# Order of TensorE's queue in a two-block transformer kernel: dense steps of 8 products, patient mixer steps, RWKV head pairs dealt 3 + 1

## The chip, the cores and the metric

The kernel runs on one core of a Trainium2 chip. The metric is the device time of one execution in microseconds; lower is better. Every time below is of the whole program.

## The reference

512 tokens of width 1024 go through two blocks, all in float32.

Block 1: `h = rmsnorm(x)`, one projection `h @ w_in` (1792 columns for RWKV, 1536 for attention, 2048 for gates). An RWKV-7 mixer works on 8 heads of 64, as four head pairs: a state of 64 x 64 per head is updated token by token,

```
S_t = S_{t-1} diag(w_t) + (S_{t-1} a_t) b_t^T + v_t k_t^T ;  y_t = S_t r_t
```

followed by a group norm, a bonus term and a gate; its result, 512 wide, is `o_a`. A differential attention with 4 heads (two softmaxes of 64-wide queries and keys each, causal, with ALiBi) gives `o_b`. Then

```
merged = sigmoid(g_a) * (o_a @ w_proj_a) + sigmoid(g_b) * (o_b @ w_proj_b)
x = x + merged @ w_out
x = x + square(relu(rmsnorm(x) @ w_ff1)) @ w_ff2          # 1024 -> 4096 -> 1024
x = x + (p @ w_ple) * sigmoid(rmsnorm(x) @ w_ple_gate)
```

Block 2 has the same frame with other mixers: gated linear attention (GLA, 4 heads, keys of 128, values of 256) and a dilated window attention with three groups of 4 heads of 128, merged by their log-sum-exp. A last rmsnorm gives the output.

## The kernel before

**Data.** Activations lie transposed, features on the 128 partitions and 512 tokens along the row. Each dense product is done in float32r in three parts: the weight and the activation are both split into a high and a low half, and `hi*hi`, `hi*lo`, `lo*hi` are summed in one PSUM bank. The halves of activations are called XH and XL (OAH/OAL for the RWKV result, OBH/OBL for the attention result, MH/ML, OGH/OGL, OTH/OTL, mid, YH/YL elsewhere), those of weights wh and wl. Weights come by DMA from SP's queue into two raw buffers (NRAW = 2), ScalarE rounds them into wh (lane "hi"), VectorE subtracts into wl (lane "lo"); there are three buffers of each. Mixer matmuls (scores, transposes against the identity, RWKV and GLA steps) are in plain float32, and the hardware does each of them as more than one matmul record.

**Lanes and steps.** The program is written as generators, one for each chain of work on each engine: a lane. Everything between two `yield`s is a step, the smallest thing that is put into a queue as a whole. TensorE has six lanes (`tensor_lanes`): "norms", "sums", "scores", "a", "b" and "dense". `rehearse` runs every generator once and notes, for each step, its waits, its operations with an estimated duration, and its signals. `arrange` then plays all engines against each other with these estimates: it takes the engine that can start soonest, and of its lanes whose next step is ready the one with the smallest due value. For TensorE that is a fixed priority, norms -7, sums -6, scores -5, a -4, b -3, dense 0. So before the change any mixer step that is ready when a step ends goes ahead of the next dense step. `write` puts the instructions out in the order found. At run time each queue is in order, and an instruction waits only for its semaphores.

**Dense work** (`pe_dense`). A product of one 128-column weight unit with 8 feature slices is 24 matmuls of 128 x 512: `upper` does hi*hi and hi*lo for each slice k, and yields before every second k; `under` does lo*hi and yields before every fourth. A step is thus 4 matmuls. Products with weights of 4 slices (`w_proj_a`, `w_proj_b`) have 12. `tm`, which is used where the result must have tokens on partitions (values for the attentions, and the last gate), has steps of 6. The order of products in block 1 is: RWKV columns, attention values, queries and keys of two heads, gates, queries and keys of the other two, gates; then pairs of gate products ("gb") alternating with products of the attention result OBH, OBL ("pb"); then the four of the RWKV result OAH, OAL ("pa"); then `w_out`, the MLP, the gate.

**RWKV.** `pe_prep` has six to eight steps for each of the four head pairs (LD,LS; bones; ident; rkw; AR,BT), in lanes a and b by turns. A block inverse on VectorE follows. Then two workers (`pe_worker`, lanes a and b, each with two PSUM banks and eleven pages of its own) go through items: one item is one head pair and one half of the tokens. In an item TensorE does, in this order and each waiting for an evacuation of the one before: AR,KT (two steps), AR,BT (two), transposes ident,AR and ident,V, the last item's output (ident,T or ident,SQ, with GD,G), transposes ident,BT and ident,KT, VT,AKR, then X,UB, G,NB, X,UB, then ARB,UA with BP,UA, then UA,BP with VT,KP, then up to four state steps SB,MP, and the output UA,ARB, VT,AKR, SB,AR. Most of these use 64 rows or 64 columns of the array. The items are in `WORK` (line 21): pairs 0 and 1 for worker 0, pairs 2 and 3 for worker 1. Worker 0 waits for the inverse. Worker 1 uses pages and banks of the attention and waits for its end: `at("l", "OB", 3)`, which is the last OBL, and the last score's maximum.

**Attention.** `pe_scores` has 32 steps (AQ, 64 rows, 128 to 512 columns), all in one bank, each waiting until VectorE has taken the last. `pe_sums` transposes the probabilities (ident,AP) and multiplies by the values (AV,PT); `pe_attn_norm` (ident,scan) turns a finished head. In block 2 `pe_gla_prep`, `pe_gla_mix`, `pe_dil_scores` (DQ) and `pe_dil_sum` (ident,P and PTD,DVT) are in the same lanes.

Of the kernel before, what the change touches and what calls it, by code (L numbers as in the profile page):

```python
# [17 lines left out]
NEG = -3.0e38  # L18
C_DECAY = float(np.exp(-0.5))
GN_EPS = 64 * 1e-5  # L20
WORK = ((0, 1), (2, 3))
# [199 lines left out]
class Lane:  # L221
    def __init__(self, stream, name, write, slack):
        self.stream, self.name, self.write, self.slack = stream, name, write, slack
        self.steps, self.unit_of, self.i, self.gen = [], [], 0, None


class Kernel:
# [162 lines left out]
    def upper(self, s, u, j, x, key, k0, k1):  # L390
# [4 lines left out]
        for k in range(k0, k1):  # L395
            if k % 2 == 0 and k > k0:
                yield
            w = u["hi"][:, k, 128 * j:128 * j + 128] if both is None else both[:, k, :]
            o = bank[:, :] if both is None else bank[0:48, :]
            pe.wait_ge(self.at("hi" if both is None else "lo", u["i"]), self.at("h", x, k))  # L400
            pe.matmul(o, w, self.x[x][0][k], k == 0, False)
            pe.wait_ge(self.at("l", x, k))
            i = pe.matmul(o, w, self.x[x][1][k], False, both is not None and k == u["kk"] - 1)
            self.mm += 2
            if both is not None and k == u["kk"] - 1:
                i.then_inc(*s.up(("acc",) + key, ("wfree", u["i"])))

    def under(self, s, u, j, x, key, k0, k1):
# [3 lines left out]
        for k in range(k0, k1):  # L412
            if k % 4 == 0:
                yield
# [626 lines left out]
    def pe_prep(self, s, i):  # L1041
        pe, bank = self.pe, self.ps[4 + i % 2]
# [161 lines left out]
    def pe_worker(self, s, w):  # L1204
        pe, b, at = self.pe, self.W[w], self.at
# [325 lines left out]
    def pe_scores(self, s):  # L1531
        pe, bank = self.pe, self.ps[6]
        last = [("begin", 6)]
# [45 lines left out]
    def pe_sums(self, s):  # L1579
        pe, at, bank, ob = self.pe, self.at, self.ps[7], self.ps[3]  # L1580
        free = [("begin", 7)]
# [774 lines left out]
    def pe_gla_prep(self, s, h):  # L2356
        pe = self.pe
        yield
# [58 lines left out]
    def pe_gla_mix(self, s):  # L2417
        pe, at, bank = self.pe, self.at, self.gla_bank
        for h in range(4):
# [119 lines left out]
    def pe_dil_scores(self, s):  # L2539
        pe, at = self.pe, self.at  # L2540
        for g in range(3):
# [321 lines left out]
    def rehearse(self):  # L2863
        for eng, stream, lanes in (("pe", self.pe, self.tensor_lanes), ("dv", self.dv, self.vector_lanes), ("ac", self.ac, self.scalar_lanes),
                                   ("pl", self.pl, self.pool_lanes), ("sp", self.sp, self.sync_lanes)):
            self.order[eng] = []
            for name, slack, write in lanes():
                self.splitting = 0
# [3 lines left out]
                while more:  # L2872
# [6 lines left out]
                    lane.unit_of.append(self.splitting)  # L2879
                self.lanes.append(lane)  # L2880
# [4 lines left out]
    def arrange(self):  # L2885
# [26 lines left out]
        while any(left.values()):  # L2912
# [9 lines left out]
            start, eng, go = best  # L2922
# [9 lines left out]
            lane = min(go, key=due)[1]  # L2932
            now, stream = start, streams[eng]
            for note in lane.steps[lane.i]:
# [85 lines left out]
```

## Time and profile before

| | |
|---|---|
| runs shown | 1953.95, 1956.66, 1958.48 us; median 1956.66 |
| profiled execution | 1953.57 us, its span from first to last instruction 1951.8 us |
| TensorE busy, mean granted clock | 1928.2 us, 0.997 |
| TensorE's weight loads (beside its matmuls) | 1580.0 us |
| VectorE, ScalarE, GpSimdE busy | 1017.2, 738.6, 99.9 us |
| matmul records | 9550 |

The duration of one matmul in the rows (389 ns for a dense one) is from its start to its end in a pipeline: the next starts before it ends. What a stretch costs is read from starts. "x4" in a timeline row is a group of neighbours of one kind, its first start and the time to its last end. Mixer tiles are named by what they hold; buffer numbers are left out, so both workers' tiles have one name (the output page is T for worker 0, SQ for worker 1).

### The profile page before, as it was taken

What the parts mean: (1) busy time and instruction counts of PE and PEld (TensorE: products, weight loads), DVE (VectorE), ACT (ScalarE), POOL (GpSimd) and SP (SyncE); (2) the same over time, 40 slices, a digit from 0 to 9 for tenths busy, and PEclk for the clock granted to TensorE, in tenths of its full rate; (3) what the DMA queues carried; (4) which work ended last, traced back from release to release, by engine and by line L of the source; (5) the groups of instructions that cost most, each with busy time, mean ns of one, the idle gap of its engine ahead of it and who ended that gap; (6) DMA issues with size and microseconds to landing.
All of it is one profiled execution on the core that took longest, in us unless ns stands there. A gap on an engine that the chain in (4) does not pass through costs nothing.

```text
span 1951.8 us, 23333 instructions
## 1 busy us (share of the span) xinstructions
PE 1928.2 (99%) x9550; PEld 1580.0 (81%) x9550; DVE 1017.2 (52%) x1717; ACT 738.6 (38%) x1184; POOL 99.9 (5%) x155
## 2 busy tenths in 40 slices
PE   7999999999999999999999999999999999999997
PEld 6787778778888888888788888898888888888886
DVE  5768574446754444466834435424345644444544
ACT  6434454333433223234734233333233432313233
POOL 2000111102000000000101000000000000000000
PEclk9999999999999999999999999999999999999999
DMA  6232310226343233232432222231354332322321
GB/s 223 65 103 95 82 46 29 65 76 234 102 149 99 96 97 98 96 99 76 142 98 64 74 80 84 91 107 64 110 194 141 97 108 87 108 86 87 108 87 43
DMA packets 174557, 194.65 MB, mean 100 GB/s; under 512 B 14825, under 2 KB 151699, under 8 KB 174450
## 3 DMA queue, kind: packets, MB, share of 16 engines
q1 hardware_dynamic: 167794, 179.82, 28.8%
q0 software_dynamic: 5072, 11.03, 1.7%
q10 hardware_dynamic: 1584, 2.30, 0.3%
q8 instruction: 76, 1.25, 0.3%
q14 instruction: 31, 0.25, 0.0%
HBM read 179.41 MB, written 15.54 MB: 100 GB/s over the span
## 4 chain that ended last, share of the span: by engine, by line
PE 95%; DVE 2%; ACT 2%; DMA 1%; issue 0%; POOL 0%; ACTq 0%; POOLq 0%; DVEq 0%
PE bank L130 93%; PE bank L133 2%; ACT L140 0%; DMA scr_x<-XT 0%; DVE XL L162 0%; DVE XT L162 0%; ACT GP L140 0%; DVE wl L154 0%; DMA g_rows<-in_norm_mix_g_dram 0%; ACT xt L140 0%; DVE KI L154 0%; DVE GP L162 0%; ACT LD L140 0%; DVE GP L177 0%; POOL scr_x L118 0%
## 5 line engine op out<-in xcount | busy, mean ns | idle before, releaser
L140 ACT ACTIVATE wh<-raw 128x1024 fp32r<-128x1024 f32 (+1 forms) x299 | 316.0, 1057 | 709.7 <-PE bank L130 706.0
L130 PE MATMUL bank<-XH,wh 128*128 128x512 f32 (+1 forms) x1272 | 507.7, 399 | 3.0 <-DVE XL L162 2.2
L130 PE MATMUL bank<-XL,wh 128*128 128x512 f32 (+1 forms) x1272 | 497.0, 391 | 0.0
L154 DVE TENSOR_TENSOR wl<-raw,wh 128x1024 fp32r<-128x1024 f32 x298 | 365.2, 1226 | 228.6 <-ACT wh L140 227.9
L130 PE MATMUL bank<-XH,wl 128*128 128x512 f32 x1264 | 324.3, 394 | 0.0
L130 PEld LDWEIGHTS bank<-XH,wh 128*128 128x128 f32 (+1 forms) x1272 | 239.1, 188 | 60.4 <-issue 5.2
L130 PEld LDWEIGHTS bank<-XL,wh 128*128 128x128 f32 (+1 forms) x1272 | 239.2, 188 | 47.9
L130 PEld LDWEIGHTS bank<-XH,wl 128*128 128x128 f32 x1264 | 233.5, 188 | 51.9 <-issue 4.1
L130 PE MATMUL bank<-mid,wh 128*128 128x512 f32 x1024 | 243.8, 389 | 0.0
L130 PEld LDWEIGHTS bank<-mid,wh 128*128 128x128 f32 x1024 | 192.2, 188 | 39.9
L154 DVE TENSOR_TENSOR T<-bank,RST 128x512 f32<-128x512 f32 x122 | 84.1, 689 | 234.2 <-PE bank L130 234.0
L130 PE MATMUL bank<-mid,wl 128*128 128x512 f32 x512 | 127.7, 389 | 0.0
L130 PEld LDWEIGHTS bank<-mid,wl 128*128 128x128 f32 x512 | 96.1, 188 | 20.0
L154 DVE TENSOR_TENSOR T<-T 128x512 f32<-128x512 f32 (+1 forms) x68 | 45.1, 673 | 88.2 <-ACT T L140 88.1
L140 ACT ACTIVATE T<-bank 128x512 f32<-128x512 f32 x64 | 37.1, 592 | 115.2 <-PE bank L130 115.2
L130 PE MATMUL bank<-wh,XH 128*128 128x512 f32 x192 | 60.3, 395 | 0.0
L130 PE MATMUL bank<-wl,XH 128*128 128x512 f32 x192 | 59.8, 392 | 0.0
L130 PE MATMUL bank<-wh,XL 128*128 128x512 f32 x192 | 59.7, 392 | 0.0
L154 DVE TENSOR_TENSOR XT<-XT,T 128x512 f32<-128x512 f32 x72 | 49.8, 691 | 2.1
L130 PE MATMUL bank<-OGH,wh 128*128 128x512 f32 x128 | 50.1, 391 | 0.0
L130 PE MATMUL bank<-OGL,wh 128*128 128x512 f32 x128 | 49.8, 389 | 0.0
L154 DVE TENSOR_TENSOR T<-T,bank 128x512 f32<-128x512 f32 (+1 forms) x40 | 26.3, 658 | 41.0 <-PE bank L130 26.0
(426 smaller groups left out, 2319.3 us busy)
## 6 DMA issues: line engine op xcount, KB each, us to landing
raw<-in_w_in_dram SPq DMA_DIRECT2D x58, 1024.0 KB, 5.3
raw<-in_w_ff_dram SPq DMA_DIRECT2D x32, 1024.0 KB, 5.3
raw<-in_w_mlp_dram SPq DMA_DIRECT2D x32, 1024.0 KB, 5.3
raw<-in_w_out_dram SPq DMA_DIRECT2D x8, 1024.0 KB, 5.6
scr_x<-XT POOLq DMA_DIRECT2D x16, 256.0 KB, 4.9
XT<-scr_x SPq DMA_DIRECT2D x8, 512.0 KB, 8.0
raw<-in_w_ple_gate_dram SPq DMA_DIRECT2D x4, 1024.0 KB, 5.3
raw<-in_w_o_gla_dram SPq DMA_DIRECT2D x4, 1024.0 KB, 5.3
```

The source lines that it names most:

```text
L130: return self.put(ns, lambda e: e.matmul(out, lhsT, rhs, start=start, stop=stop, skip_group_check=True))
L133: return self.put(109, lambda e: e.transpose(out, in_, ident))
L140: return self.put(ns, lambda e: e.activation(out, in_, func, bias=bias, scale=scale), func)
L154: return self.put(self.ns(out), lambda e: e.tensor_tensor(out, a, b, op))
```

## The change

Four things are changed, all of them in what the planner is given or how it picks.

- `upper` yields before every fourth k and `under` before every eighth, so a dense step of a product on 8 slices is 8 matmuls. `tm` is as it was.
- Every step of a TensorE lane has a patience, noted at the rehearsal: `PATIENCE = (2000, 4000, 0)` ns, the first for attention in block 1 (scores and sums), the second for the mixers of block 2, the third for the RWKV preparation; 0 for the workers and the norms. If TensorE's last step was dense and a dense step is ready, the dense one is taken as long as every other ready step has been ready for less than its patience. Once a mixer step has been taken the old rule holds: mixer steps go on as long as one is ready.
- The planner adds 90 ns to TensorE's clock at each change between dense and mixer steps. This is in the plan only, no instruction is issued.
- `WORK` gives pairs 0, 1 and 3 to worker 0 and pair 2 to worker 1.

```diff
--- before.py
+++ after.py
@@ -16,9 +16,10 @@
 BASE = 16512
 PAGE = 2048
 NEG = -3.0e38
+PATIENCE = (2000, 4000, 0)
 C_DECAY = float(np.exp(-0.5))
 GN_EPS = 64 * 1e-5
-WORK = ((0, 1), (2, 3))
+WORK = ((0, 1, 3), (2,))
 C128 = 128.0 ** -0.5
 LAM_INIT = 0.8 - 0.6 * float(np.exp(-0.3 * 0))
 
@@ -221,7 +222,7 @@
 class Lane:
     def __init__(self, stream, name, write, slack):
         self.stream, self.name, self.write, self.slack = stream, name, write, slack
-        self.steps, self.unit_of, self.i, self.gen = [], [], 0, None
+        self.steps, self.unit_of, self.patience, self.i, self.gen = [], [], [], 0, None
 
 
 class Kernel:
@@ -393,7 +394,7 @@
         if k0 == 0:
             pe.wait_ge(*[self.at(*e) for e in self.bank_after[key]])
         for k in range(k0, k1):
-            if k % 2 == 0 and k > k0:
+            if k % 4 == 0 and k > k0:
                 yield
             w = u["hi"][:, k, 128 * j:128 * j + 128] if both is None else both[:, k, :]
             o = bank[:, :] if both is None else bank[0:48, :]
@@ -410,7 +411,7 @@
         if k0 == 0 and j == 0:
             self.need_lo[u["i"]] = self.mm
         for k in range(k0, k1):
-            if k % 4 == 0:
+            if k % 8 == 0:
                 yield
             pe.wait_ge(self.at("lo", u["i"]))
             i = pe.matmul(bank[:, :], u["lo"][:, k, 128 * j:128 * j + 128], self.x[x][0][k], False, k == u["kk"] - 1)
@@ -1039,6 +1040,7 @@
             dv.tensor_tensor(self.LL[r[x], :], self.WA[r[x], :], self.LD[x][r[x], :].bitcast(F32), ALU.subtract).then_inc(*s.up(("ll",)))
 
     def pe_prep(self, s, i):
+        self.patient = PATIENCE[2]
         pe, bank = self.pe, self.ps[4 + i % 2]
         pb, cs = self.prep_pages[i % 2][1], slice(128 * i, 128 * i + 128)
         for x, (name, free) in enumerate((("zw", ("abe", i - 2, 1) if i >= 2 else ("pv",) if i == 0 else ("rst0",)), ("za", ("sg", i)))):
@@ -1202,6 +1204,7 @@
         return [(i, hf) for i in self.W[w]["todo"] for hf in range(2)]
 
     def pe_worker(self, s, w):
+        self.patient = 0
         pe, b, at = self.pe, self.W[w], self.at
         ARB, AKR, BP, KP, VT, MP, X, G, UA, UB, NB, SB = [b[n] for n in ("ARB", "AKR", "BP", "KP", "VT", "MP", "X", "G", "UA", "UB", "NB", "SB")]
         B0, B1 = b["banks"]
@@ -1530,6 +1533,7 @@
 
     def pe_scores(self, s):
         pe, bank = self.pe, self.ps[6]
+        self.patient = PATIENCE[0]
         last = [("begin", 6)]
         for h, b in self.items:
             n = 128 * (b + 1)
@@ -1578,6 +1582,7 @@
 
     def pe_sums(self, s):
         pe, at, bank, ob = self.pe, self.at, self.ps[7], self.ps[3]
+        self.patient = PATIENCE[0]
         free = [("begin", 7)]
         for x in range(17):
             if x < 16:
@@ -2355,6 +2360,7 @@
 
     def pe_gla_prep(self, s, h):
         pe = self.pe
+        self.patient = PATIENCE[1]
         yield
         pe.wait_ge(self.at("hasl"), self.at("free", "ha"), self.at("wasl"), *([self.at("p1", h - 2)] if h >= 2 else [self.at("browc", h)]))
         pe.matmul(self.ps[6 + h % 2][:, :], self.WAS[:, 128 * h:128 * h + 128], self.HAS[:, :], True, True).then_inc(*s.up(("zb", h)))
@@ -2416,6 +2422,7 @@
 
     def pe_gla_mix(self, s):
         pe, at, bank = self.pe, self.at, self.gla_bank
+        self.patient = PATIENCE[1]
         for h in range(4):
             vs = slice(256 * h, 256 * h + 256)
             yield
@@ -2538,6 +2545,7 @@
 
     def pe_dil_scores(self, s):
         pe, at = self.pe, self.at
+        self.patient = PATIENCE[1]
         for g in range(3):
             for h in range(4):
                 qk = self.DQ[h % 2]
@@ -2865,7 +2873,7 @@
                                    ("pl", self.pl, self.pool_lanes), ("sp", self.sp, self.sync_lanes)):
             self.order[eng] = []
             for name, slack, write in lanes():
-                self.splitting = 0
+                self.splitting = self.patient = 0
                 lane = Lane(eng, name, write, slack)
                 sig, gen = self.sig(f"{eng}_{name}"), None
                 gen, more = write(sig), True
@@ -2877,6 +2885,7 @@
                         more = False
                     lane.steps.append(stream.notes)
                     lane.unit_of.append(self.splitting)
+                    lane.patience.append(self.patient)
                 self.lanes.append(lane)
         self.rehearsing = False
         for sig in self.sigs.values():
@@ -2930,7 +2939,15 @@
                     return max(t, clock["pe"]) + 227 * (need[l.unit_of[l.i]] - dense) - lead
                 return t + l.slack
             lane = min(go, key=due)[1]
+            if eng == "pe":
+
+                was = self.order[eng][-1] if self.order[eng] else lane
+                dense_lane = [l for _, l in go if l.name == "dense"]
+                if was.name == "dense" and dense_lane and all(start - t < l.patience[l.i] for t, l in go if l.name != "dense"):
+                    lane = dense_lane[0]
             now, stream = start, streams[eng]
+            if eng == "pe" and (lane.name == "dense") != (was.name == "dense"):
+                now += 90
             for note in lane.steps[lane.i]:
                 if note[0] == "wait":
                     sem, value = place[note[1]] if note[2] is None else (note[1].name, note[2])
```

## Rows read from the trace of the kernel before

**Rows 1.** The page: its first line, TensorE's busy share, its granted clock by slice.

```profile
span 1951.8 us, 23333 instructions
...
PE 1928.2 (99%) x9550; PEld 1580.0 (81%) x9550; DVE 1017.2 (52%) x1717; ACT 738.6 (38%) x1184; POOL 99.9 (5%) x155
...
PEclk9999999999999999999999999999999999999999
```

**Rows 2.** Waits of TensorE over the span: us in total, times, longest.

```profile
PE bank L133 <- DMA g_rows<-in_norm_mix_g_dram: 5.1, 1, 5.1
```

**Rows 3.** TensorE's timeline, end of the RWKV mixer: start us, us, what.

```profile
447.36 0.39 PE L130 MATMUL bank<-OBH,wh 128*128 128x512 f32 x1
...
450.10 0.39 PE L130 MATMUL bank<-OBH,wh 128*128 128x512 f32 x1
...
456.22 0.39 PE L130 MATMUL bank<-OAH,wh 128*128 128x512 f32 x1
```

**Rows 4.** TensorE's timeline from 308 us: worker 0's state steps between dense runs.

```profile
311.78 0.33 PE L130 MATMUL bank<-SB,MP 64*64 64x64 f32 x4
...
313.17 0.33 PE L130 MATMUL bank<-SB,MP 64*64 64x64 f32 x4
```

**Rows 5.** TensorE's timeline from 337 us: a state step between other worker steps.

```profile
338.54 0.33 PE L130 MATMUL bank<-SB,MP 64*64 64x64 f32 x4
338.80 0.34 PE L130 MATMUL bank<-UA,BP 128*64 128x64 f32 x4
```

**Rows 6.** TensorE's timeline from 281 us: dense matmuls between two score steps.

```profile
283.75 0.50 PE L130 MATMUL bank<-XH,wh 128*128 128x512 f32 x1
...
285.79 1.12 PE L130 MATMUL bank<-AQ 64*128 64x512 f32 x2
```

**Rows 7.** TensorE's timeline in block 2, from 1044 us.

```profile
1046.79 1.03 PE L130 MATMUL bank<-GV,KOT 128*128 128x256 f32 x4
1047.47 0.58 PE L130 MATMUL bank<-XH,wh 128*128 128x512 f32 x1
...
1049.51 0.59 PE L130 MATMUL bank<-GV,KOT 128*128 128x256 f32 x2
1049.94 1.04 PE L133 MATMUL bank<-ident,T 128*128 128x128 f32 x8
```

**Rows 8.** Tiles OBH, OBL and OAL: ns min/median/max, first and last start, forms.

```profile
L130 PE MATMUL bank<-OBH,wh x32: 387/396/583, 377.4 to 454.9; 128*128 128x512 f32 x32
...
L162 DVE SCALAR_TENSOR_TENSOR OBL<-bank,sg,OBH x4: 741/745/753, 215.0 to 303.2; 128x512 fp32r<-128x512 f32 x4
...
L154 DVE TENSOR_TENSOR OAL<-SQ,OAH x4: 424/426/426, 365.8 to 456.0; 128x256 fp32r<-128x256 f32 x4
```

**Rows 9.** TensorE's timeline: AR,KT at the start of three items of worker 1.

```profile
314.56 0.54 PE L130 MATMUL bank<-AR,KT 64*64 64x128 f32 x5
...
385.29 0.65 PE L130 MATMUL bank<-AR,KT 64*64 64x128 f32 x8
...
415.78 0.65 PE L130 MATMUL bank<-AR,KT 64*64 64x128 f32 x8
```

**Rows 10.** TensorE's groups by form from 211 to 456 us: busy us, mean ns.

```profile
L130 PE MATMUL bank<-XH,wh 128*128 128x512 f32 x120 | 51.2, 426 | 0.0
...
L130 PE MATMUL bank<-OBH,wl 128*128 128x512 f32 x32 | 9.1, 405 | 0.0
```

**Rows 11.** Tiles SS and OTL: first and last start.

```profile
L130 PE MATMUL bank<-SS,QD x24: 379/379/379, 1033.0 to 1064.4; 128*128 128x256 f32 x24
...
L154 DVE TENSOR_TENSOR OTL<-bank,OTH x4: 690/692/692, 1321.1 to 1359.9; 128x512 fp32r<-128x512 f32 x4
```

**Rows 12.** TensorE from 14 to 16 us: us, busy (count), granted clock, DMA.

```profile
14.00:16.00 2.00, 2.00 (x7) 0.50 1.13 325
```

## The prediction

> **What bounds the kernel now.** I read the page's busy shares and slices first, then TensorE's waits, then TensorE's timeline around its changes of work, and last the tiles that carry work from one stage to the next. TensorE is busy in 99% of the span, in every slice after the first, at full granted clock [rows 1]. Its waits are a handful, all but one in the first microseconds or in block 2, the longest 5.1 us [rows 2]. So the time is the work in TensorE's queue plus what it loses where it changes from one kind of work to another. Of its 9550 matmuls 7264 are dense ones, which start every 0.227 us when they follow each other (twelve of them from 447.36 to 450.10 us take 2.74, 0.228 each [rows 3]). That is 1649 us. I call the runs of other matmuls between them excursions; counted in TensorE's timeline over the whole span there are 174.
>
> What does an excursion cost beyond its matmuls? It depends on its kind.
> - A state step of a worker, SB,MP (64 x 64), alone between dense runs: a step at 311.78, the next at 313.17 [rows 4]. One period is 313.17 - 311.78 = 1.39 us, of which four dense matmuls are 0.91, which leaves 0.48. The same step between steps of its own kind takes 338.80 - 338.54 = 0.26 us [rows 5]. So leaving and coming back costs 0.22 us.
> - A score step, AQ (64 rows): eight dense matmuls from 283.75 to 285.79 take 2.04 us where 8 x 0.227 = 1.82 [rows 6]: 0.22 us again.
> - A step on the whole array (128 rows and columns) in block 2: eight dense from 1047.47 to 1049.51 take 2.04 us, again 0.22 too long, but the step before them, four matmuls of 256 columns, takes only 1047.47 - 1046.79 = 0.68 where its own pitch (1049.51 to 1049.94: two in 0.43) gives 0.86 [rows 7]. The sum is 0.22 - 0.18 = 0.04 us.
>
> I take 0.21 us for an excursion with half-array steps and 0.04 for one without. By my count in the timeline 87 of the 174 hold a half-array step: 14 in the RWKV preparation (37 to 135 us), 16 in attention alone (162 to 211), 32 while worker 0 runs (211 to 348), 25 after that. All of block 2's are whole-array. What the excursions cost is therefore about 87 x 0.21 + 87 x 0.04 = 21.8 us, 1.1% of the time. That is a ceiling; no edit here removes a matmul.
>
> The rows also show why. The Trainium skill (TensorEngine Tiling (Array Packing), Key Properties) says that a change of tiling mode drains TensorE, while another tile of the same mode doesn't. By that rule the price is on changes of mode and not on excursions, and patience in block 2, where no mode changes, buys nothing; the trace agrees (0.04 against 0.22 us). At a flat 0.18 us for each excursion, as the planner books it now (90 ns each way), block 2's part below would be 4.5 us and not 1.
>
> **The change part by part.** Matmuls, their operands, the DMAs and the other engines' instructions stay; what changes is the order in each queue, TensorE's above all.
>
> *Dense steps of 8.* A dense product on 8 slices was six steps of 4 matmuls and is three of 8. The planner can leave it at half as many places: a worker step that is ready after 4 matmuls now waits for 8, up to 0.91 us more. It removes an excursion only where two ready steps fall into one gap. Row-major products (tm) keep their steps of 6. The 90 ns that the planner adds to its clock at each change of kind issue nothing; they only shift what it takes for ready, which I price at 0, within 1 us either way.
>
> *Patience.* In block 1 a score or sums step waits until it has been ready for 2.0 us if the planner is in dense work and nothing else is due; in block 2 all mixer steps wait 4.0 us; preparation, workers and norms don't wait. From 162 to 211 us only attention runs: the score steps come 2.5 to 3.5 us apart on average; with a wait of 2.0 us and steps of 1.82 us they come two dense steps and their own 0.4 to 1.1 us apart, about 4.9 us. So 49 us hold some 10 excursions for 16, which saves 6 x 0.21 = 1.3 us; four of the 32 score steps slide behind 211 us, where they ride along with worker steps.
>
> *Pairs 3 + 1.* Worker 1 can't start before attention ends, as its pages and banks are attention's: the last OBL is written at 303.2 to 303.9 us [rows 8] and its first AR,KT is at 314.56 [rows 9]. Now it has four half-pair items in series, the last of which is normalised into OAL at 456.0 to 456.4; the product that needs it starts at 456.2 [rows 3, 8]. From 348 us on worker 1 runs alone, in 25 half-array excursions. After the change worker 0 goes on with pair 3 beside worker 1's pair 2: two items beside each other took 7 excursions between 314.5 and 348 us, one alone takes 12 (counted from its first step at 385.29 to the next item at 415.78 [rows 9]; 8 of the 12 are half-array). So the 25 become 6 + 8, and a few for norms, about 15: 10 x 0.21 = 2.1 us.
>
> *Sum.* Preparation: two or three of 14 merge as two lanes share it, 0.5 us; attention 1.3; 211 to 348 us: 32 to about 29, 0.6; after that 2.1. Half-array excursions go from 87 to some 66, 4.5 us. Whole-array ones (11 to 40 fewer, most in block 2) save 25 x 0.04 = 1.0 us at most, and I take 0.3, since those with a half-array neighbour still pay its price. In all 4.8 us. The bounds: 1 us if merging pairs half-array with whole-array steps only, 8 us if 40% of the half-array excursions go and most of block 2's too.
>
> **Does a wait take its place?** The dense work is what fills TensorE while a mixer step is evacuated. From 211.3 to 456.2 us there are 124 + 2 x 120 + 3 x 32 = 460 dense matmuls, in six rows of which the first and the last stand in [rows 10]. They then meet two gates.
> - *OBH, OBL at 377.4 us* [rows 8] need attention's end, at 303.9 now: 73 us of slack. Afterwards attention ends later: four score steps late at 4 to 5 us each, and longer gaps, so about 320 to 335 us. The gate comes sooner, since the 268 dense matmuls before it go by in runs of 8: some 35 are done already by 211 us (the mixers' 4 to 5 us that slid, and 3 us of later preparation), and the other 233 are 29 runs, which at 3.7 to 4.5 us each with their excursion give 321 to 345 us. The slack is nearly gone; I price a miss at 0 to 6 us of idle.
> - *OAH, OAL at 456.2 us* need the last worker item and its norm. Item alone: 30.5 us from 385.29 to 415.78 [rows 9], of it 68 dense matmuls (15.4 us) in 12 runs, seven of 4 and five of 8. With every run at 8 it is 15.1 + 12 x 1.82 = 36.9 us. From 211 to 314.5 us there are 35 runs and 176 matmuls; at 8 each for all, 280, 24 us more. The pair of items beside each other: 33.5 us with 7 runs, 5.7 us more. End of the chain at the worst: 211 + 3 (preparation) + 103 + 24 + 2 x 39 + 37 + 10 (norm) = 466 us. But that takes no run away; long runs let more steps get ready, and a run that bridges a latency already is not made longer. With a third of the added time gone that way (24 + 11 + 6 = 41 becomes 27) it is 452. The dense work alone gets there at 456.2 - 4.5 = 451.7. So the two meet, as they do now with 1 us between them. Because the matmuls behind the gate don't depend on any of this, only the gate's moment counts: idle is 0 to 11 us.
>
> In block 2 the waits lengthen chains with room: GLA's mix has its last SS,QD at 1064 and OGH is first used at 1334; OTL is written by 1360 and the first OTH product is at 1431.7 [rows 11].
>
> Queued behind: SP's loads of the alibi page wait for a head's scores, and the next weight loads stand behind them; POOL's memsets for worker 1 wait for the last OBL, with the norm powers of worker 0 behind. If attention is later than the planner has it, both queues stand. I price it at 0, covered by two raw weight buffers, each of which lasts two units, 48 x 0.227 = 10.9 us, and at 3 us if that cover is gone.
>
> **How the time comes out.** Profiled execution before: span 1951.8, its time 1953.57, of which 1.8 lies around the span. 1953.57 - 4.8 + 0.3 for idle at the second gate = 1949.1. The median of the runs shown is 1956.66, 3.1 above the profiled one: 1952.2, so 1952.
>
> **Rivals.**
> 1. *The gates eat it.* Idle of 2 to 6 us at either gate, savings of 3 to 5: 1954 to 1960, mostly within 0.2% (3.9 us, about what a measurement of this kernel tells from no change). For it: both slacks shrink to a few us by the sums above. Against: worker steps don't wait by the rule, and the 3 + 1 deal takes two items off the late starter.
> 2. *Slower: the RWKV chain holds the product on OA.* Six items in series on worker 0, each 6 us longer, end at 462 to 466 us; the gate opens 6 to 10 us after 456.2 and everything behind it moves by that. 1956.7 + 6 to 10 = 1963 to 1967. It decides as soon as the last OAL is later than about 460 us, that is if less than a seventh of the 41 us above is saved by merging. For it: 12 runs per item are forced by the chain itself. Against: in the trace of before two items side by side need hardly more dense work than one. An idle TensorE could also lose clock: from 14 to 16 us, after the first waits, the granted clock was 0.50 (the lower level, 1.2 GHz) and the 2 us held five dense starts (the row counts two more that were under way), where 0.227 us apart it would be nine [rows 12]; I give that 1 to 2 us more.
> 3. *Nothing merges.* Half- and whole-array steps meet, so the changes of mode stay: 1 us saved, 1955 to 1956. The Trainium skill's rule on tiling modes (TensorEngine Tiling (Array Packing), Key Properties) is for this one.
>
> **Chances.** Forecast case (saving 4 to 8, no gate late) 0.47; gates eat it 0.21; nothing merges 0.11; slower by the chain or the OB gate 0.21. Faster than 0.2% 0.47, same 0.32, slower 0.21. The range 1944 to 1963 takes in 8 us saved, with room for the scatter of the medians (the three runs shown lie 4.5 us apart), and the slower case's lower end; about 0.09 lies above and 0.08 below. The likeliest case alone: 1946 to 1953.
>
> **What would show it.** Right: excursions down from 174 to about 125 to 140, those with half-array steps to about 66; AQ steps mostly two dense steps apart before 211 us; worker 0's KT,AR running on to about 410; TensorE's busy share 99% with no wait over 1 us at the first OBH or OAH. Wrong: a wait of TensorE on OBL or OAL or on a step of the worker between 320 and 460 us, OAH starting after 456.2, or a dense pitch other than 0.227 us.

## The result, and the profile after

| | before | after |
|---|---|---|
| median | 1956.66 us (1953.95 to 1958.48, 5 runs) | 1948.59 us (1947.35 to 1952.46, 5 runs) |
| profiled execution, span | 1953.57, 1951.8 us | 1947.35, 1945.5 us |

The ratio is 0.9963, 95% interval [0.9948, 0.9978]: faster, by 8.1 us in the medians and by 6.3 us in the two profiled spans. The forecast was a median of 1952 us. Executions of one kernel lie up to 10 us apart (r3's 16), so below the lowest time of a kernel stands beside its median. One execution of e1, at a mean granted clock of 0.751, took 2399.5 us and is left out of every comparison.

The page after, its first line, TensorE's busy share and its granted clock by slice, against [rows 1]: the same number of matmuls, the same clock, 6.3 us less of busy TensorE.

```profile
span 1945.5 us, 23335 instructions
...
PE 1921.9 (99%) x9550; PEld 1582.4 (81%) x9550; DVE 1018.8 (52%) x1717; ACT 740.1 (38%) x1186; POOL 97.8 (5%) x155
...
PEclk9999999999999999999999999999999999999999
```

Waits of TensorE after (us in total, times, longest), against [rows 2]. The first and longest one is the one of before. None names a tile of either gate, OBL or OAL.

```profile
PE bank L134 <- DMA g_rows<-in_norm_mix_g_dram: 5.3, 1, 5.3
PE bank L131 <- DVE XL L163: 2.2, 1, 2.2
PE bank L134 <- DVE AP L163: 1.3, 2, 0.9
```

TensorE's timeline at the end of the mixer stretch, against [rows 3]. Twelve dense matmuls take 451.01 - 448.29 = 2.72 us, 0.227 each as before; the first product on OAH starts at 451.01 where it started at 456.22.

```profile
448.29 0.39 PE L131 MATMUL bank<-OBH,wh 128*128 128x512 f32 x1
...
451.01 0.39 PE L131 MATMUL bank<-OAH,wh 128*128 128x512 f32 x1
```

So 5.2 of the 6.3 us are gained ahead of that product, although the first matmul of all starts 0.25 us later than before (5.34 and 5.09 us). Behind it before took 1951.8 - 456.2 = 1495.6 us and after 1945.5 - 451.0 = 1494.5: the other 1.1 us, in block 2.

The tiles at the two gates (ns min/median/max, first and last start), against [rows 8]. The last OBL starts at 306.2 us and the first OBH product at 370.6: 64 us of room. The last OAL starts at 437.3 and takes 0.4, and its product starts at 451.0: 13 us of room, where before had none (456.0 and 456.2).

```profile
L131 PE MATMUL bank<-OBH,wh x32: 387/389/497, 370.6 to 449.6; 128*128 128x512 f32 x32
...
L163 DVE SCALAR_TENSOR_TENSOR OBL<-bank,sg,OBH x4: 746/748/753, 218.1 to 306.2; 128x512 fp32r<-128x512 f32 x4
...
L155 DVE TENSOR_TENSOR OAL<-T,OAH x6: 418/424/428, 250.9 to 437.3; 128x256 fp32r<-128x256 f32 x6
```

TensorE's timeline, AR,KT of the first item of worker 0, of the first of worker 1 and of the last item of all, against [rows 9]. Worker 0 begins at 200.0 us (before: 211.3), worker 1 at 316.4 (314.6).

```profile
200.00 0.68 PE L131 MATMUL bank<-AR,KT 64*64 64x128 f32 x16
...
316.35 0.68 PE L131 MATMUL bank<-AR,KT 64*64 64x128 f32 x16
...
394.93 0.71 PE L131 MATMUL bank<-AR,KT 64*64 64x128 f32 x12
```

TensorE's timeline in attention alone: the score steps now stand mostly 16 dense matmuls apart, 4.3 to 4.9 us from one to the next (the last two before 200 us are 6.7 and 3.1 us apart).

```profile
166.61 0.48 PE L131 MATMUL bank<-AQ 64*128 64x128 f32 x2
...
170.99 0.70 PE L131 MATMUL bank<-AQ 64*128 64x256 f32 x2
171.62 0.50 PE L131 MATMUL bank<-XH,wh 128*128 128x512 f32 x1
...
175.49 0.70 PE L131 MATMUL bank<-AQ 64*128 64x256 f32 x2
```

Counted in TensorE's timeline as before, excursions fall from 174 to 115, those with half-array steps from 87 to 62:

| us | half-array excursions before | after |
|---|---|---|
| 37 to 135 | 14 | 13 |
| 162 to 211 | 16 | 11 |
| 211 to 348 | 32 | 23 |
| 348 to 446 | 25 | 15 |

By the prediction's prices that is 25 x 0.21 + 34 x 0.04 = 6.6 us, against 6.3 measured.

The mixers of block 2 (first and last start), against [rows 11]: later by 17 and 34 us, and still ahead of the products that need them; OTL is read from 1425.7 us on.

```profile
L131 PE MATMUL bank<-SS,QD x24: 379/379/379, 1036.2 to 1081.4; 128*128 128x256 f32 x24
...
L155 DVE TENSOR_TENSOR OTL<-bank,OTH x4: 691/692/693, 1318.5 to 1393.6; 128x512 fp32r<-128x512 f32 x4
```

### The profile page after: what moved, and what is told of

Same layout as the page of the kernel before. It is cut to its first block, busy times and chain, and to the rows that moved or that the text cites. A ratio compares the mean times of both kernels' runs of the same rounds, so it can differ in the third digit from the quotient of the medians.

```text
span 1945.5 us, 23335 instructions
## 1 busy us (share of the span) xinstructions
PE 1921.9 (99%) x9550; PEld 1582.4 (81%) x9550; DVE 1018.8 (52%) x1717; ACT 740.1 (38%) x1186; POOL 97.8 (5%) x155
## 4 chain that ended last, share of the span: by engine, by line
PE 96%; ACT 2%; DVE 1%; DMA 1%; issue 0%; POOL 0%; ACTq 0%; DVEq 0%
PE bank L131 94%; PE bank L134 2%; DMA scr_x<-XT 0%; ACT L141 0%; DVE XL L163 0%; ACT GP L141 0%; DMA g_rows<-in_norm_mix_g_dram 0%; DVE wl L155 0%; ACT wh L141 0%; ACT xt L141 0%; POOL scr_x L119 0%; ACT LD L141 0%; ACT AP L142 0%; DVE KI L155 0%; ACT T L141 0%
## 5 line engine op out<-in xcount | busy, mean ns | idle before, releaser
L131 PE MATMUL bank<-XH,wl 128*128 128x512 f32 x1264 | 317.7, 392 | 0.0
```

The costliest lines, as they stand in the source:

```text
L131: return self.put(ns, lambda e: e.matmul(out, lhsT, rhs, start=start, stop=stop, skip_group_check=True))
```

## The experiments

Three questions: is the price on the change between half and whole array (the prediction's account) or on every excursion; which of the edits brings the gain; and how near is the kernel to the chain of RWKV items (rival 2)? Twelve runs; kernels in one table part ran on one chip beside the kernel before.

The expectations name accounts of the price by letters. A: 0.21 us for an excursion with half-array steps, 0.04 for one without, as predicted. B: a flat 0.107 us for each. C: the deal alone is worth nothing. D: the price is on each change between half-array and whole-array matmuls. In r1 to r4, which were written last, "A" is what D was, at 0.2 us a change, and "A0" is the A of before.

| kernel | median us | lowest us | ratio to before, 95% |
|---|---|---|---|
| before (23 runs) | 1954.72 | 1952.37 | |
| e1: before, pairs 3 + 1 | 1952.69 | 1949.48 | 0.9986 [0.9977, 0.9995] |
| e2: before, dense steps of 8 | 1961.63 | 1961.36 | 1.0040 [1.0028, 1.0052] |
| e3: after, pairs 2 + 2 | 1961.38 | 1959.15 | 1.0034 [1.0021, 1.0047] |
| e4: after, no patience | 1948.01 | 1947.41 | 0.9973 [0.9961, 0.9985] |
| before (1 run) | 1956.07 | | |
| q1 to q4: probes | 2069.44, 2123.20, 2070.47, 2175.30 | | one run each |
| before (17 runs) | 1956.08 | 1952.46 | |
| r1: after again | 1948.17 | 1946.60 | 0.9964 [0.9952, 0.9977] |
| r2: scores wait 5 us | 1946.71 | 1945.57 | 0.9957 [0.9945, 0.9969] |
| r3: workers wait 2 us | 1992.37 | 1981.36 | 1.0181 [1.0156, 1.0206] |
| r4: without the 90 ns | 1956.43 | 1953.76 | 1.0006 [0.9995, 1.0016] |

### What an excursion costs: q1 to q4

Each adds the same 1024 matmul records of 128 columns (512 matmuls, whose results are overwritten) to the kernel before, in the MLPs, where there are no mixers: on 128 rows of the identity (q1, q3) or 64 rows (q2, q4); four matmuls at one place of a product, or two at two places. q2 against q1 has 128 half-array excursions for 128 whole-array ones; q3 and q4 have 256.

```
+    def probe(self, u, n):
+        if u["name"] in ("f1", "f2"):
+            for x in range(n):
+                self.pe.matmul(self.ps[3][:, 128 * x:128 * x + 128], self.ident[0:64, :], self.ident[0:64, :], x == 0, True)   # q1, q3: 0:128
+            self.mm += n
...
             if k % 4 == 0:
                 yield
+            if k == 0:
+                self.probe(u, 4)      # q3, q4: 2 here and 2 in upper at k == 4
```

> A measurement of the price itself: the kernel before, with four extra plain float32 matmuls of 128 x 128 by 128 (identity by identity, into a bank that nobody reads then) in each of the 128 products of the two MLPs, ahead of its lo*hi part; their result is not used. All use the whole array. In the mixers such a group of four takes 0.91 us and costs 0.01 to 0.1 on leaving and coming back. Theories A and D: span longer by 128 x (0.90 + 0.02) = 117 us. Flat price of 0.107 (theory B): 128 x (0.90 + 0.107) = 128 us.

> As the whole-array probe, but with 64 of the 128 rows: four matmuls of 64 x 128 by 128 at each of the 128 places. Theory B: as long as with the whole array. Theories A and D: longer than it by the price of a half-array excursion, 128 x 0.21 = 27 us, or up to 128 x 0.38 = 49 us if the AR,BT steps of the preparation show it (8 records in 1.29 us, against 0.91 for 8 on the whole array).

> As the whole-array probe with the same number of extra matmuls, but dealt to two places in each product, two and two (256 excursions for 128). Theories A and D: 128 x 0.04 = 5 us longer than all four at one place, or less. Theory B: 128 x 0.107 = 14 us longer.

> As the half-array probe, dealt two and two. This is gathering undone, 128 times. Theories A and D: 27 to 49 us longer than all four at one place. Theory B: 14 us longer.

Spans, one execution each: q1 2067.7, q2 2121.4, q3 2068.7, q4 2173.5 us (the kernel before beside them 1954.3). q1 is 113.4 us longer, where A and D said 117 and B 128. q2 - q1 = 53.7 us for 128 excursions made half-array, 0.42 each. q4 - q2 = 52.1 for 128 more half-array ones, 0.41 each. q3 - q1 = 1.0 for 128 more whole-array ones, 0.008 each. The spans also differ ahead of the probes: the first product on OAH starts at 456.07, 457.75, 455.54 and 455.74 us. From there to the end the same differences are 52.1, 54.1 and 1.5 us, or 0.41, 0.42 and 0.012 each. The half-array price lies above the widest expectation (0.38). A flat price is refuted: an excursion that stays on the whole array is nearly free here. TensorE's timeline shows one of each. In q1:

```profile
705.95 1.05 PE L130 MATMUL bank<-ident 128*128 128x128 f32 x8
706.76 2.07 PE L130 MATMUL bank<-XH,wl 128*128 128x512 f32 x8
708.67 0.39 PE L130 MATMUL bank<-XH,wh 128*128 128x512 f32 x1
```

708.67 - 705.95 = 2.72 us is just 8 x 0.113 + 8 x 0.227. In q2, counted from the last dense matmul before it:

```profile
705.10 0.39 PE L130 MATMUL bank<-XL,wh 128*128 128x512 f32 x1
705.42 1.16 PE L130 MATMUL bank<-ident 64*128 64x128 f32 x8
706.51 2.11 PE L130 MATMUL bank<-XH,wl 128*128 128x512 f32 x8
708.46 0.39 PE L130 MATMUL bank<-XH,wh 128*128 128x512 f32 x1
```

3.36 us for 0.227 + 2.72 = 2.95: 0.41 too much, spread over the way in (705.10 to 705.42: 0.09 over a pitch), the first steps inside, and the way out. The price of the prediction, 0.21, was half of that. The reason is in its yardstick: the 0.26 us of a state step "between steps of its own kind" [rows 5] ran from SB,MP (64 x 64) to UA,BP (128 x 64), another form, and held a change itself. TensorE's timeline of e4 has eight state matmuls as one group,

```profile
350.64 0.45 PE L131 MATMUL bank<-SB,MP 64*64 64x64 f32 x8
```

0.45 us from first start to last end where four take 0.33 [rows 5]: 0.12 for four more. With that in place of 0.26 the excursion of [rows 4] costs 1.39 - 0.91 - 0.12 = 0.36. The prediction's second case, the score step, had the same gap: [rows 6] was read on the dense side alone, and what the step itself loses was left out, though it was counted for block 2. In the changed kernel two AQ matmuls of 256 columns hold TensorE from 170.99 to 171.62, 0.63 us, where two of 256 columns on the whole array take 0.43 [rows 7]: 0.20 too long. The 16 dense ones up to 175.49 take 3.87 us where 16 x 0.227 = 3.63: another 0.24. Together that is 0.44.

Why then does 0.21 fit the change (6.6 against 6.3)? Two errors cancel. Counted in TensorE's timeline ahead of the first product on OAH, the changes between dense and half-array matmuls fall from 142 to 92, which is 25 round trips. But those between half-array and whole-array mixer steps, inside the excursions, rise from 109 to 139: a merged excursion often holds both. (Changes between two unlike half-array forms stay, 31 and 34.) So 10 round trips go on balance, 4.1 us at 0.41. The planner's order says the same, 252 changes between half and whole array before and 232 after.

The starts bear this out. Summed from each start to the next, the 1104 dense matmuls ahead of that product take 277.3 us before and 268.4 after, 8.9 less; the mixer matmuls between them take 173.9 and 177.3, 3.4 more. That makes 5.5 us, of which the 10 round trips are 4.1. The other 1.4 us, and the 1.1 in block 2, go along with 34 fewer whole-array excursions, 0.07 us each. That is a remainder and not a measured price; q3 has 0.012 for such an excursion of identity matmuls.

### The parts alone: e1, e2, e3

**e1**, the kernel before with the new deal only (150 excursions, 74 half-array, by its order; 174 and 88 before).

```
-WORK = ((0, 1), (2, 3))
+WORK = ((0, 1, 3), (2,))
```

> The kernel before, with the 3 + 1 deal of the head pairs alone (dense steps of 4, no patience). Counted in TensorE's queue as it is written, excursions go from 174 (88 with half-array steps, 86 without) to 150 (74 and 76). Theory A, a price of 0.21 us for an excursion with half-array steps and 0.04 for one without: 14 x 0.21 + 10 x 0.04 = 3.3 us less. Theory B, a flat price for every excursion (the change took 59 away for 6.3 us of span, 0.107 each): 24 x 0.107 = 2.6 us less. Theory C, that the deal only repairs what the longer dense steps break and is worth nothing alone: 0. OAH's first matmul: 3 us sooner than 456.2 by A, with the last OAL far earlier than now.

2.0 us under before in the medians, 2.9 in the lowest times. There is no trace of it at full clock, so only its times are used. They refute C. They fit A (14 x 0.21 + 10 x 0.04 = 3.3) and B (2.6) alike: the interval spans 1.0 to 4.5 us.

**e2**, the kernel before with the new dense steps only (144 excursions, 72 half-array).

```
-            if k % 2 == 0 and k > k0:
+            if k % 4 == 0 and k > k0:
...
-            if k % 4 == 0:
+            if k % 8 == 0:
```

> The kernel before, with dense steps of 8 alone (old deal, no patience). Excursions 144 (72 with half-array steps, 72 without) for 174 (88, 86). Theory A without idle: 16 x 0.21 + 14 x 0.04 = 3.9 us less. Theory A with my rival 2, that four items in series on worker 1 after attention's end reach the product on OA late: each item 6 us longer, 317 + 4 x 36.9 + 10 = 475 us for the last OAL against about 452 for the dense work, less what merges, so 8 to 20 us of idle before OAH's first matmul, and the time 4 to 16 us above before. TensorE's waits in the trace decide between them.

Its excursions promised 3.9 us (16 x 0.21 + 14 x 0.04); it is 7 to 9 us slower instead. This is rival 2. TensorE's timeline of e2 has the last dense group of the stretch at 443.89, then the last item's steps with nothing between them, then the norm:

```profile
443.89 1.17 PE L130 MATMUL bank<-OBH,wl 128*128 128x512 f32 x4
444.90 1.08 PE L130 MATMUL bank<-G,NB 128*128 128x128 f32 x8
446.69 1.16 PE L130 MATMUL bank<-X,UB 128*128 128x128 f32 x8 [0.71 <-ACT X L140]
448.63 0.44 PE L130 MATMUL bank<-ARB,UA 128*64 128x128 f32 x4 [0.78 <-DVE UA L154]
...
451.42 0.33 PE L130 MATMUL bank<-SB,MP 64*64 64x64 f32 x4 [0.50 <-ACT SB L140]
...
456.68 1.12 PE L130 MATMUL bank<-SB,AR 128*64 128x128 f32 x8
462.60 0.69 PE L133 MATMUL bank<-ident,SQ 128*128 128x128 f32 x2 [4.80 <-DVE SQ L154]
463.08 1.06 PE L130 MATMUL bank<-GD,G 128*128 128x256 f32 x2
463.58 0.99 PE L130 MATMUL bank<-OAH,wh 128*128 128x512 f32 x1
```

The product on OAH starts at 463.58, 7.4 us after that of [rows 3]. In those 19.7 us TensorE waits 7.8 us for its own evacuations, of which 4.8 for the norm (SQ) alone. It also loses its clock, and does so before that longest wait, as stretches of 4 us show (TensorE's busy us and count; granted clock; DMA share, GB/s):

```profile
448.00:452.00 4.00, 2.62 (x56) 1.00 0.00 0
452.00:456.00 4.00, 3.26 (x28) 0.81 0.00 0
456.00:460.00 4.00, 1.80 (x14) 0.50 0.00 0
460.00:464.00 4.00, 1.40 (x5) 0.50 0.01 4
464.00:468.00 4.00, 4.00 (x11) 0.50 0.18 50
468.00:472.00 4.00, 4.00 (x18) 0.98 1.01 354
```

0.50 is the lower of the two levels, 1.2 GHz of 2.4; the dense matmuls behind the gate run at it until 468 us (0.43 us from one start to the next).

**e3**, the changed kernel with the old deal (127 excursions, 69 half-array).

```
-WORK = ((0, 1, 3), (2,))
+WORK = ((0, 1), (2, 3))
```

> The changed kernel with the old deal (pairs 0, 1 and 2, 3), all else as changed. Excursions 127 (69 with half-array steps, 58 without). Theory A with rival 2: 19 x 0.21 + 28 x 0.04 = 5.1 us saved and 8 to 20 us of idle before OAH's first matmul, so 3 to 15 us slower than before. If the deal is only a means to fewer excursions: 5 us faster than before, 1 us slower than the changed kernel, no idle.

The same end as e2, though its worker 0 starts 12 us sooner (200.7 against 212.6). The steps of worker 1 alone, after attention's end, set it. TensorE's timeline of e3:

```profile
462.63 0.69 PE L134 MATMUL bank<-ident,SQ 128*128 128x128 f32 x2 [4.80 <-DVE SQ L155]
...
463.61 0.99 PE L131 MATMUL bank<-OAH,wh 128*128 128x512 f32 x1
```

So the deal is worth 2 to 3 us with dense steps of 4, and 12 to 13 with steps of 8 (1959.15 against 1947.35 and 1946.60 in the lowest times). Dense steps of 8 alone are a loss. With the deal they paid only in an order that was planned with the 90 ns, as r4 below shows.

### Patience: e4, r2, r3

**e4**, the changed kernel without patience (137 excursions, 67 half-array; changes 226).

```
-PATIENCE = (2000, 4000, 0)
+PATIENCE = (0, 0, 0)
```

> The changed kernel with every patience at 0 (dense steps of 8, 3 + 1 deal, the planner's 90 ns stay). Excursions 137 (67 with half-array steps, 70 without) for 115 (63 and 52) in the changed one. Theory A: patience is worth 4 x 0.21 + 18 x 0.04 = 1.6 us, so 4.7 us less than before in the span. Theory B (flat 0.107): 22 x 0.107 = 2.4 us, so 3.9 less than before. Theory D, that the price is on changes between half-array and whole-array matmuls (226 here, 232 in the changed kernel, 252 before): patience is worth nothing or a little less, this kernel 5 to 6 us less than before. The three differ by less than the medians' scatter; the spans by stage and the moment of OAH's first matmul are read for it.

No difference from the changed kernel can be told in the times (1948.01 against 1948.59 and 1948.17; lowest 1947.41 against 1947.35 and 1946.60). Behind the first product on OAH (456.5 us in a span of 1952.1, after a fall of the clock at 363 us) e4 takes 1495.6 us, as before does; the changed kernel takes 1494.5 in both its profiled executions (1949.4 - 454.9 in r1). So patience in block 2 is worth 1.1 us, for 14 whole-array excursions fewer than before (50 to 36 behind 455 us). In block 1 it does something the prediction didn't have: it keeps attention's work on VectorE, which evacuates the scores and does the softmax, out of the way while the inverse runs there. Between the first and the last step of the inverse VectorE executes 119 instructions before and 97 after; of these 43 and 23 are attention's (11.6 and 5.4 us; in r2 10, 2.1 us), and its idle time falls from 4.2 to 0.9 us. The evacuation of the scores from 145 to 185 us, before and after:

```profile
L180 DVE CUSTOM_DVE_ANT_0 AP<-bank,ALB 128x128 f32<-128x128 f32 (+3 forms) x7 | 3.2, 457 | 1.1 <-PE bank L130 1.1
```

```profile
L181 DVE CUSTOM_DVE_ANT_0 AP<-bank,ALB 128x128 f32<-128x128 f32 (+2 forms) x5 | 2.0, 396 | 0.7 <-PE bank L131 0.7
```

The inverse's steps on VectorE (first and last start) in before, e4, after and r2, in this order:

```profile
L154 DVE TENSOR_TENSOR IU<-IU,IW x31: 192/359/425, 145.3 to 193.1; 128x31 f32<-128x31 f32 x2, 128x60 f32<-128x60 f32 x2, 128x87 f32<-128x87 f32 x2, 128x112 f32<-128x112 f32 x2
```

```profile
L155 DVE TENSOR_TENSOR IU<-IU,IW x31: 192/358/425, 144.2 to 189.8; 128x31 f32<-128x31 f32 x2, 128x60 f32<-128x60 f32 x2, 128x87 f32<-128x87 f32 x2, 128x112 f32<-128x112 f32 x2
```

```profile
L155 DVE TENSOR_TENSOR IU<-IU,IW x31: 192/358/426, 143.7 to 182.3; 128x31 f32<-128x31 f32 x2, 128x60 f32<-128x60 f32 x2, 128x87 f32<-128x87 f32 x2, 128x112 f32<-128x112 f32 x2
```

```profile
L155 DVE TENSOR_TENSOR IU<-IU,IW x31: 192/359/424, 142.9 to 178.7; 128x31 f32<-128x31 f32 x2, 128x60 f32<-128x60 f32 x2, 128x87 f32<-128x87 f32 x2, 128x112 f32<-128x112 f32 x2
```

From first to last start that is 47.8, 45.6, 38.6 and 35.8 us, and worker 0 starts at 211.3, 205.4, 200.0 and 195.7. The other runs agree: 47.9 us in e2, without patience (worker 0 at 212.6), and 38.7 in e3, with it (200.7).

**r2**, scores wait 5 us (110 excursions, 55 half-array, changes 210).

```
-PATIENCE = (2000, 4000, 0)
+PATIENCE = (5000, 4000, 0)
```

> The changed kernel as it is, as the base for the next three. Its order has 115 excursions, 63 of them with half-array steps, and 232 changes between half-array and whole-array matmuls (before: 174, 88, 252). Its lowest time so far is 1947.35 us, that of the kernel before 1952.4 to 1953.3. Theory A (what counts is the changes between half and whole array, 0.2 us each, plus 0.04 for a whole-array excursion): 20 x 0.2 + 36 x 0.04 = 5.4 us under before at equal clock. Theory A0 (0.21 us for every excursion with a half-array step, as predicted): 25 x 0.21 + 36 x 0.04 = 6.7 us under.

> The changed kernel with patience 5 us for the attention's score and sums steps instead of 2 us: 110 excursions, 55 with half-array steps, 210 changes between half and whole array. Against the changed kernel: A 22 x 0.2 + 0 = 4.4 us less, about 1943 us; A0 8 x 0.21 - 3 x 0.04 = 1.6 us less, about 1946; if the longer waits make attention end so late that the product on OBH waits or the RWKV workers start late, equal to it or slower (1948 to 1955), with a wait of TensorE on OBL or on a worker's tile.

r1 is 5.9 us under before in the lowest times, between the two accounts (A 5.4, A0 6.7). r2 speaks against A: 1.0 us under r1 (1.5 in the medians), where A says 4.4 and A0 1.6. The product on OAH starts at 449.2 us in r2, 1.8 before the 451.0 of the changed kernel, of which 0.9 is there already at the first dense matmul (13.1 and 14.0 us). The intervals of r1 and r2 overlap, so that r2 is faster is likely and not shown. Its times are the lowest of the study.

Why did 22 changes buy only 1 us? The timeline ahead of OAH has 19 fewer between dense and half-array matmuls (73 for 92) and 3 fewer between half and whole array inside the excursions (136 for 139), but 14 more between unlike half-array forms (48 for 34), which A leaves out. By SB,MP such a change costs 0.26 - 0.12 = 0.14 us, so an estimate is 22 x 0.205 - 14 x 0.14 = 2.5 us. The rest is open.

**r3**, workers wait 2 us (98 excursions, 51 half-array).

```
     def pe_worker(self, s, w):
-        self.patient = 0
+        self.patient = 2000
```

> The changed kernel with patience 2 us for the workers' steps too (0 before): 98 excursions, 51 with half-array steps, 216 changes. A: 16 x 0.2 = 3.2 us less at best; A0: 12 x 0.21 = 2.5 less. The changed kernel has 13 us between the last OAL (437.8 us) and the first product on OAH (451.0). Rival (the RWKV chain is what pays): six items of worker 0 in series, each with some 12 runs of dense work, wait up to 1.8 us more in a part of them, 20 to 40 us in all; the last OAL comes at 458 to 478 us, the dense work in front of it runs out at 448, the steps left then run bare, and the time is 1955 to 1970.

36 us slower than before, with the fewest excursions of all. The last OAL starts at 492.7 us, against 437.3. TensorE's longest groups of waits (us, times, longest), and the clock over the stretch:

```profile
PE bank L131 <- ACT SB L141: 6.8, 10, 1.7
PE bank L134 <- DVE T L155: 5.5, 2, 4.8
```

```profile
446.00:470.00 24.00, 18.54 (x150) 0.64 0.01 2
```

The direction was expected; the 1981 to 1998 us is beyond the range of 1955 to 1970, since the chain grew by 55 us, not 20 to 40, and ran bare from 418 us, where the last OBH product starts, to 490.7, in good part at 1.2 GHz (0.64 of the full clock from 446 to 470 us).

### The planner's 90 ns: r4

```
             if eng == "pe" and (lane.name == "dense") != (was.name == "dense"):
-                now += 90
+                now += 0
```

> The changed kernel without the 90 ns that the planner adds to its clock of TensorE at a change between dense and mixer steps: 127 excursions, 69 with half-array steps, 236 changes. A: 4 x 0.2 = 0.8 us more than the changed kernel, within the scatter; A0: 6 x 0.21 + 6 x 0.04 = 1.5 us more. If that bookkeeping matters through readiness (steps thought ready earlier or later than they are), TensorE's waits on worker tiles differ by more than 1 us from the changed kernel's.

Both sums are wrong: 7.2 us slower than r1 in the lowest times (8.3 in the medians), level with before. The last part of the expectation came true, that TensorE's waits on worker tiles differ by more than 1 us. So the whole gain of the change hangs on an order that the other three edits without the 90 ns don't give. The 127 excursions are not the reason (+1.5 us); the chain is. Worker 0 starts at 213.0 us (before: 211.3), the dense work runs out at 459 and TensorE waits for the norm. TensorE's timeline:

```profile
458.19 1.08 PE L131 MATMUL bank<-OBH,wl 128*128 128x512 f32 x4
462.93 0.55 PE L134 MATMUL bank<-ident,T 128*128 128x128 f32 x2 [3.66 <-DVE T L155]
...
463.77 0.99 PE L131 MATMUL bank<-OAH,wh 128*128 128x512 f32 x1
```

The last OAL starts at 465.8 us, 28.4 later than in the changed kernel. 13.0 of these are worker 0's late start. The inverse begins 7.6 us later (151.3 for 143.7) and takes 2.4 longer, and then SP's queue issues its reload (UC) 8.5 us after its store (192.6 and 201.1 us), in the changed kernel 2.7 (182.5 and 185.2). The other 15.4 us are the chain's own length. Why this order has them was not tried.

## Why the prediction was right

The forecast was 4.8 us saved and a median of 1952; measured were 6.3 us in the spans, 8.1 in the medians, and 1948.6. The mechanism and the sign held: fewer half-array excursions at an unchanged pitch, no wait at either gate. The size came out near by luck, as the price of a half-array round trip was half of what it is, and the changes that merging leaves inside the excursions stood in the lower bound alone and not in the sum. Step by step:

- **Price of an excursion.** 0.21 and 0.04 us give 6.6 for the counted excursions, 6.3 measured. As the price of one round trip between whole and half array, 0.21 is wrong: alone it is 0.41. It fits the change only because 15 of the 25 round trips saved at the dense matmuls come back between mixer steps.
- **Preparation** 0.5 us; one excursion went, 0.2.
- **Attention alone** 1.3 us from 6 fewer; 5 went, 1.1. Its steps are mostly 4.3 to 4.9 us apart, where 4.9 was forecast.
- **211 to 348 us** 0.6 us from 3 fewer; 9 went, 1.9. This was sized too small: I let pairs of workers merge as before, and the earlier start of worker 0 together with runs of 8 gives them more to share (argued, not tried apart).
- **After 348 us** 2.1 us from 10 fewer; 10 went.
- **Whole-array excursions** 0.3 us taken, 1.0 at most; 34 went, 1.4 by the price, of which 1.1 is shown in block 2.
- **Gate on OBH.** I had attention end at 320 to 335 us and the gate at 321 to 345. It ends at 307 and the gate comes at 370.6. Both terms failed. For attention I let four score steps slide at 4 to 5 us each, but its last one starts at 283.8 us, before at 286.3.
- **Gate on OAH.** Chain end 452 forecast, 437.8 found. Its length was right: 238 us from a start at 214 forecast, 237.8 from 200.0 found. The start was wrong by 14 us, by the inverse on VectorE (e4, r2), a term that the prediction did not have. Without it the "two meet" of the forecast would have been close to true.
- **The 90 ns at 0, within 1 us.** Wrong: 7 us (r4), through the order that it leads to.

**Rivals.** 1, gates eat it: no, 64 and 13 us of room. 2, the chain holds the product on OA: not here, but it is real and near. e2, e3, r3 and r4 all fall to it, with OAH at 463.6, 463.6, 490.7 and 463.8 us. For the lost clock I gave 1 to 2 us: from OAH to the end e2 takes 3.1 us more than before (1498.7 against 1495.6), e3 and r4 1.5 and 0.9 more than the changed kernel. 3, nothing merges: 62 half-array excursions for 87 refute it as it stands, but its reason holds in part, as half-array and whole-array steps do meet in one excursion (139 such changes for 109). The Trainium skill's rule (TensorEngine Tiling (Array Packing), Key Properties), a change of tiling mode drains TensorE and another tile of the same mode doesn't, the probes bear out, 0.41 against 0.01 us. That patience in block 2 would then buy nothing, as I took from it, is not what the runs show: it bought 1.1 us where no mode changes (e4).

## What to carry to other kernels

On a full engine, price an interruption by its form: find from raw starts what one round trip costs, on both sides of the change, and check that the yardstick row holds no change of form itself. Count the changes that a merged interruption still holds inside. And count the merges only after the slack of the longest dependent chain is known: each edit that fills gaps with longer dense steps also lengthens that chain (e2: 4 us of merges promised, 7 to 9 us lost), and an edit that shortens or splits the chain is what makes the filling pay. Bookkeeping constants of a planner are edits too, and are to be measured like one.

## What the runs showed of the hardware

A change from dense matmuls to four on 64 rows and back cost 0.41 to 0.42 us (q1 to q4), for a score step of 256 columns 0.44; to four whole-array matmuls of the identity and back it cost 0.01 us.

The granted clock also falls where TensorE is hardly idle. r1 is the changed kernel itself; its profiled execution took 1951.23 us. TensorE in stretches of 4 us (the two before, from 352 to 360 us, were busy throughout at 1.00):

```profile
360.00:364.00 4.00, 3.93 (x37) 0.84 0.02 4
364.00:368.00 4.00, 4.00 (x26) 0.50 0.00 0
368.00:372.00 4.00, 4.00 (x24) 0.81 0.00 0
```

Its product on OAH comes at 454.9 us and not at 451.0, which is the whole difference of the two executions (1949.4 and 1945.5 us of span); 0.9 us of it is there before the fall, from the first 45 us on, and 3.0 come with it. What ran in the 10 us before the fall were mostly the workers' small steps (UA,ARB; VT,AKR; SB,AR; SB,MP; AR,KT) and eight dense matmuls. In e4 it fell at the same place, in e2, r4 and r3 at 253, 258 and 323 us. In the execution shown as after, the same queue went through there at 1.00, so the order alone doesn't decide it; what does is open.
